# A gate projection by seven half products ahead of the convolution projection, and one weight mixture moved from VectorE to GpSimd

## The reference, cut to what matters

```python
h = rmsnorm(x, norm_mix)
cb, cc, cu, q, k, v, g, ga, gb = split(h @ w_in)
y_conv = (cb * conv3(cc * cu)) @ w_conv_out
y_ret = retention(q, k, v, g) @ w_ret_out
merged = sigmoid(ga) * y_conv + sigmoid(gb) * y_ret
x = x + merged @ w_o
h2 = rmsnorm(x, norm_mlp)
x = x + square(relu(h2 @ w_up)) @ w_down
```

## Time and profile before

| | |
|---|---|
| median of 3 executions | 2114.24 us (2113.4 to 2114.38) |
| the profiled execution | 2116.72 us, span 2114.9 us |
| granted clock of PE, mean | 0.996 of full speed |
| PE busy | 2088.9 us, 99% |
| DVE busy | 1531.7 us, 72% |
| ACT busy | 1017.3 us, 48% |
| POOL busy | 1.4 us |
| chain that ended last | PE 80%, DVE 5%, ACT 1% |

### The profile page before, as it was taken

How to read it: one execution, slowest core, us unless ns; L and a number is a source line. 1 busy time by engine, 2 the same in 40 slices (tenths; PEclk the granted TensorE clock), 3 DMA queues, 4 the chain that set the end, 5 groups by cost and what they waited for, 6 DMA issues and landing times.

```text
span 2114.9 us, 29718 instructions
## 1 busy us (share of the span) xinstructions
PE 2088.9 (99%) x11940; PEld 1869.0 (88%) x11950; DVE 1531.7 (72%) x2096; ACT 1017.3 (48%) x1456; POOL 1.4 (0%) x6
## 2 busy tenths in 40 slices
PE   9999999999999999999999999999999999999997
PEld 8888878878888899988999998888899988999996
DVE  8787785758756888756876776756779756776785
ACT  5776574645434355334553453434354334553452
POOL 0000000000000000000000000000000000000000
PEclk9999999999999999999999999999999999999998
DMA  5333222213222223422332333222223422332332
GB/s 184 110 100 101 88 80 71 90 65 100 100 80 80 86 84 120 139 90 90 120 110 87 123 110 108 92 80 80 90 81 120 140 90 90 120 110 90 120 113 77
DMA packets 59544, 212.15 MB, mean 100 GB/s; under 512 B 6736, under 2 KB 7120, under 8 KB 59280
## 3 DMA queue, kind: packets, MB, share of 16 engines
q1 hardware_dynamic: 59040, 208.83, 28.9%
q0 software_dynamic: 224, 1.31, 0.2%
q10 hardware_dynamic: 144, 0.12, 0.0%
HBM read 208.14 MB, written 2.10 MB: 99 GB/s over the span
## 4 chain that ended last, share of the span: by engine, by line
PE 80%; DVE 5%; ACT 1%; issue 1%; DMA 0%; DVEq 0%; ACTq 0%
PE bank L804 17%; PE bank L806 17%; PE bank L805 17%; PE bank L847 6%; PE bank L849 6%; PE bank L851 6%; PE bank L799 2%; PE bank L800 2%; PE bank L801 2%; DVE w_lo L1816 1%; PE bank L1050 1%; PE bank L1042 1%; ACT arena L1600 0%; PE bank L1120 0%; PE bank L1119 0%
## 5 line engine op out<-in xcount | busy, mean ns | idle before, releaser
L1816 DVE TENSOR_TENSOR w_lo<-w_raw,w_hi 128x1024 fp32r<-128x1024 f32 x459 | 551.5, 1215 | 416.6 <-ACT w_hi L1219 414.2
L1219 ACT ACTIVATE w_hi<-w_raw 128x1024 fp32r<-128x1024 f32 x459 | 474.5, 1048 | 626.9 <-PE bank L806 482.3
L804 PE MATMUL bank<-y_hi,w_hi 128*128 128x512 f32 x1048 | 399.6, 381 | 5.4 <-DVE y_lo L1870 3.4
L806 PE MATMUL bank<-y_hi,w_lo 128*128 128x512 f32 x1048 | 397.8, 380 | 0.0
L805 PE MATMUL bank<-y_lo,w_hi 128*128 128x512 f32 x1048 | 397.8, 380 | 0.0
L804 PE MATMUL bank<-h_both,w_hi 128*128 128x512 f32 x1020 | 389.5, 382 | 2.1 <-DVE arena L1865 1.1
L805 PE MATMUL bank<-h_both,w_hi 128*128 128x512 f32 x1020 | 386.6, 379 | 0.0
L806 PE MATMUL bank<-h_both,w_lo 128*128 128x512 f32 x1020 | 386.6, 379 | 0.0
L804 PEld LDWEIGHTS bank<-y_hi,w_hi 128*128 128x128 f32 x1048 | 198.4, 189 | 35.3 <-DVE w_lo L1816 4.5
L805 PEld LDWEIGHTS bank<-y_lo,w_hi 128*128 128x128 f32 x1048 | 198.5, 189 | 28.6 <-issue 0.7
L806 PEld LDWEIGHTS bank<-y_hi,w_lo 128*128 128x128 f32 x1048 | 198.5, 189 | 28.2
(11 more groups left out here) (302 smaller groups left out, 3258.4 us busy)
## 6 DMA issues: line engine op xcount, KB each, us to landing
w_raw<-in_stream SPq DMA_DIRECT2D x389, 512.0 KB, 3.5
x<-in_x_t SPq DMA_DIRECT2D x8, 256.0 KB, 7.3
out_t<-x SPq DMA_DIRECT2D x8, 256.0 KB, 2.2
arena<-in_consts POOLq DMA_DIRECT2D x1, 1024.0 KB, 5.2
w_raw<-in_stream SPq DMA_DIRECT2D x2, 256.0 KB, 4.6
arena<-in_positions POOLq DMA_DIRECT2D x1, 256.0 KB, 6.2
vec_t<-in_vecs ACTq DMA_DIRECT2D x1, 112.5 KB, 3.3
ident<-in_consts SPq DMA_DIRECT2D x1, 64.0 KB, 6.4
```

What stands on the lines that cost most here:

```text
L804: pe.matmul(out, w_hi[:, slot, w], streamed(a_h), start=first, stop=False)
L806: mm = pe.matmul(out, w_lo[:, slot, w], streamed(a_h), start=False, stop=last)
L1219: A.activation(w_hi[:, slot, w], w_raw[:, chunks.raw_slot[raw], w], ACT.Copy).then_inc(hi_ready, 1)
L1816: V.tensor_tensor(w_lo[:, slot, w], src[:, w], w_hi[:, slot, w].bitcast(F32), ALU.subtract).then_inc(lo_ready, 1)
```

## The change

Half 1 of both hybrid layers runs cc, cu, ga, cb, with ga by seven half products, as half 0 does; ga's weights come ahead of cb's in the stream. To make room, ga of half 1 keeps its two PSUM sums in `tmp2` (free once cu has used it, so ACT waits for that), and two of cb's convolution tiles of half 1 lie in unused rows of `y_lo`. The four scalings of z at the end of cu are left to ga (`owed`, in two pairs, paid between its remainders). merge, now directly behind cb, waits tile by tile. And in all seven-part steps, 24 before and 26 after, the mixture for T3 is made by GpSimd, with a semaphore of its own, `pooled`; it waits for the mixture of T1 and for its two chunks.

```diff
@@ schedule
-                Bind("half", 1, [*both(), s("cb", 4, 1), s("ga", 4, 1)]),
+                Bind("half", 1, [*both(), s("ga", 0, 1, seven=True), s("cb", 4, 1)]),
@@ taps_t, kept
-            return tmp2[:, n, :] if n < 2 else kept_rest[:, 2 * (T.fixed["turn"] % 2) + n - 2, :]
+            if n < 2:
+                return tmp2[:, n, :]
+            if T.var("half") == 1:
+                return y_lo_raw[:, (6 + n) * SEQ:(7 + n) * SEQ]
+            return kept_rest[:, 2 * (T.fixed["turn"] % 2) + n - 2, :]
...
+            if step.kind == "ga" and T.var("half") == 1:
+                return tmp2[:, n, :]
@@ gpsimd
+            for place, first, group in chunks.operand:
+                if place != T1:
+                    continue
+                upper, lower = (w_raw[:, chunks.raw_slot[first + i], :] for i in (1, 2))
+                for i in (1, 2):
+                    pool.wait_ge(raw_loaded[chunks.raw_slot[first + i]], 16 * chunks.raw_loads[first + i])
+                pool.wait_ge(combined, 3 * group + 1)
+                nc.gpsimd.tensor_tensor(upper, lower, upper, ALU.subtract).then_inc(pooled, 1)
@@ tensor
+            def cb(step):
+                T.mark["cb", T.var("half")] = T.value("a_lo")
+                of_h(step)
...
+                    elif step.kind == "merge" and first:
+                        pe.wait_ge(a_lo, T.mark["cb", k // 4] + k % 4 + 1)
...
-                def all_ready(k):
-                    if first and k == 0:
-                        pe.wait_ge(a_lo, T.value("a_lo"))
@@ scalar, raw_of and seven
-            made = {T1: 1, T3: 2, T2: 3, T4: 4}.get(place)
-            return raw + at, made and 4 * group + made
+            made = {T1: (combined, 3, 1), T2: (combined, 3, 2), T3: (pooled, 1, 1), T4: (combined, 3, 3)}.get(place)
+            return raw + at, made and (made[0], made[1] * group + made[2])
...
+                    if step.kind == "ga":
+                        act.wait_ge(vec, T.value("vec", -4))
                     keep(kept(T, step, 0), lent)
@@ vector, remainder
-                if place == T1:
-                    loaded(2)
-                    dve.wait_ge(combined, 4 * group + 1)
-                    V.tensor_tensor(raw[1], raw[2], raw[1], ALU.subtract).then_inc(combined, 1)
...
                 elif place == T1:
+                    loaded(2)
@@ vector, seven
-                    if kind != "up":
+                    if kind == "cc":
                         pay()
                     ahead(5)
                     pay(1)
                     ahead(6)
+                    pay(1)
                     ahead(7)
...
-                    got(4)
-                    dve.wait_ge(evacuated, T.value("turn", 4, 4))
-                    for n in range(4):
-                        z = z_pad[:, n, CONV2 - 1:]
-                        V.tensor_tensor(z, z, squared_rms, ALU.mult).then_inc(vec, 1)
+                    ready, read = T.value("vec", 4), T.value("turn", 4, 4)
+
+                    def scale(pair):
+                        dve.wait_ge(vec, ready)
+                        dve.wait_ge(evacuated, read)
+                        for n in (2 * pair, 2 * pair + 1):
+                            z = z_pad[:, n, CONV2 - 1:]
+                            V.tensor_tensor(z, z, squared_rms, ALU.mult).then_inc(vec, 1)
+
+                    owed.extend((lambda: scale(0), lambda: scale(1)))
```

More of the change, by code:

```diff
@@ L641, in build @@
         combined = sem("combined")
+        pooled = sem("pooled")
         seeded = sem("seeded")
@@ L978, in ready @@
                         pe.wait_ge(a_lo, T.mark["up", k // 4] + k % 4 + 1)
+                    elif step.kind == "merge" and first:
+                        pe.wait_ge(a_lo, T.mark["cb", k // 4] + k % 4 + 1)
                     elif first:
                         pe.wait_ge(a_lo, T.value("a_lo", k + 1 - n_k))
-                def all_ready(k):
-                    if first and k == 0:
-                        pe.wait_ge(a_lo, T.value("a_lo"))
-                product(step, lambda k: (y_hi[:, slot(k), :], y_lo[:, slot(k), :]),
-                        ready if step.kind in ("residual", "ret_proj") else all_ready)
+                product(step, lambda k: (y_hi[:, slot(k), :], y_lo[:, slot(k), :]), ready)
             def forget(step):
@@ L1168, in _ @@
                      "qk": of_h, "ret_scores": ret_scores, "ret_out": ret_out, "ret_turn": ret_turn,
-                     "g": of_h, "gb": of_h, "ret_proj": of_y, "cc": seven_products, "cu": seven_products, "cb": of_h,
+                     "g": of_h, "gb": of_h, "ret_proj": of_y, "cc": seven_products, "cu": seven_products, "cb": cb,
                      "ga": ga, "merge": of_y, "up": up, "mix": mix, "final": whole_norm}
@@ L1215, in round_raw @@
                 if made:
-                    act.wait_ge(combined, made)
+                    act.wait_ge(*made)
                 else:
```

## The result

The changed kernel takes **2119.36 us** (median of 17, 2116.45 to 2121.29), the kernel before, run in between, 2115.32 us (17 executions): ratio 1.0018, 95% interval 1.0011 to 1.0025. It is 4.0 us slower; 3.3 us faster was forecast. The profiled executions have the spans 2118.6 and 2114.9 us.

A forecast was written before the change was run, and what follows sets the result against it. PE, busy 2088.9 us (99% of the span), was taken as the bound. Terms: -3.9 (ga by seven) - 1.6 (scalings) + 2.2 (GpSimd's hold) = -3.3 us, giving a median of 2110.9 us, range 2108.2 to 2114.4.

The forecast's parts named there:

- ga by seven: ga of half 1, both layers: PE spends 18.76 instead of 20.72 us, -3.92 us in all.
- cb behind ga: Start of merge, directly after cb: tile-by-tile waits cost nothing; without them 3.5 us lost per layer.
- The scalings: cu's four scalings paid in ga: T3's w_lo comes 2.4 us sooner, half 0's 0.66 and 0.93 us go, -1.6 us.
- What GpSimd does to DVE: T1's remainder in seven-part groups: GpSimd's mixture either costs DVE nothing or holds it; 2.3 us hold taken, 1.1 later.
- the held case: GpSimd's mixture holds DVE's next instruction about 2.3 us, T1's remainder 1.1 later per group; the forecast itself, chance 0.47.
- Late next is T2 (slack 2.2), not late.: ga with the scalings paid there: after T3, T2's w_lo is next to be late, but its 2.2 us slack suffices.
- ACT's new wait: Before ga's first kept sum, ACT waits for cu's last product with the kept sum: costs nothing.
- Where 1.1 us hurts: Half 1, cu and ga: PE waits for w_lo 1.65 us in layer 0, 0.55 in layer 1, together 2.2 us.
- These hold: ga of half 0 and the six second up products (T3 slack 1.55, left 0.4): no PE waits from the delay.
- rival D: Weights come late into ga of half 1, both layers: PE waits 0.9 us more in each, 2112.7 us; chance 0.09.
- C: GpSimd holds DVE 3.35 us, 2.1 lost per group, second up product's T3 decides: +6.6 us, 2120.8; chance 0.08.
- A: GpSimd runs beside DVE, costing nothing or no more than 1.2 us; all slack stays: -5.5, 2108.7 us; chance 0.36.

The follow-up runs named there:

- the kernel with both mended: Changed kernel with T3's mixture back on DVE and ACT's first copy in ga not waiting for the deferred scalings: 2110.2 us, ratio 0.9974.
- the second experiment: Changed kernel with one wait shortened: ACT's first copy out of PSUM in ga no longer waits for DVE's four deferred scalings: 2114.31 us.
- GpSimd's mixture alone: Kernel before with only T3's mixture moved to GpSimd in all 24 seven-part steps: 2121.36 us, ratio 1.0027.
- the later mixture: Changed kernel with ACT's wait in ga shortened and GpSimd starting T3's mixture only after T2's mixture: 2112.36 us, ratio 0.9987.

## Why the prediction was wrong

**Right.** *ga by seven*: -3.9 in PE's time. *cb behind ga*: the tile-by-tile waits are worth the 3.5 us reckoned for them, per layer (one execution; in layer 0 the fall of the clock adds 1.7). *The scalings*: T3's waits of 0.66 and 0.93 in half 0 are gone. *What GpSimd does to DVE*: the held case, 2.38 us against 2.3 taken, 1.15 us per group against 1.1. That the size was hit so closely is in part luck: 2.3 was the middle between two DVE rows that say nothing of GpSimd. And the reason given for the held case, that both work through the same buffers, is not what decides: line 2609 is held without them. The Trainium skill (SBUF — State Buffer, Who interferes with whom) says that a DVE instruction with at most one SBUF input, outside the modes that use both port pairs, does not contend with GpSimd, and that one with two contends with a GpSimd instruction that reads SBUF. By that rule the trace agrees in both respects, 0.68 us for line 2604 and 2.64 for line 2609.

**"Late next is T2 (slack 2.2), not late."** This is the first step that failed: the scalings paid in ga stand in the sum with their gain of 1.6 us and no cost. I looked where DVE's queue goes and at the wait that the diff adds, but not at who else waits on the count that the moved scalings raise. ACT's new wait does cost nothing, as forecast: the kernel with both mended keeps it, and PE waits nowhere. An old wait, in no line of the diff, changed its meaning. It cost 0.88 and 0.87 us in ga of half 0, and 1.52 and 1.62 in ga of half 1: 4.9 us (5.05 by the experiment) where the sum had nothing; without GpSimd's hold it would have been 3.4. A wait in ga of half 0 was among the prediction's own signs of being wrong altogether.

**"Where 1.1 us hurts"** is the second. The delay was right; its places were not, for I had searched by the slack of `w_lo` alone. In half 1 it cost about 0.45 per layer (0.44 in the second experiment) instead of 2.2 in all: cu's T2, forecast to wait 0.8, did not wait, since the slow arrival of its first weights, 5.4 us in rows 6, did not recur. "These hold", of the up products, was wrong for the pairs of quarter 1, and the single up product of quarter 0 had not been looked at. Their parts' `w_lo` did hold (0.42 to 0.48 left in the pairs, 0.4 reckoned); ACT did not. In quarter 0 its rows are, in the changed kernel:

```profile
1010.70 1.06 ACT L1235 ACTIVATE w_hi<-w_raw 128x1024 fp32r<-128x1024 f32 x1 [3.90 <-DVE w_raw L1839]
1011.66 2.04 ACT L1748 ACTIVATE arena<-bank 128x512 f32<-128x512 f32 x4
1013.57 1.07 ACT L1235 ACTIVATE w_hi<-w_raw 128x1024 fp32r<-128x1024 f32 x1
1014.51 0.61 ACT L1270 ACTIVATE bank<-bank 128x512 f32<-128x512 f32 x1
```

The same rounding in the kernel before:

```profile
1008.76 1.06 ACT L1219 ACTIVATE w_hi<-w_raw 128x1024 fp32r<-128x1024 f32 x1 [2.66 <-DVE w_raw L1824]
```

T2's mixture comes late from DVE, ACT's rounding waits 3.90 us for it instead of 2.66, and behind it stand four copies of 0.5, another rounding, and only then the copy that PE needs. This copy starts 5.69 us into the stage instead of 4.82 (1012.58 before), and PE, which had lost 0.30 us in layer 0 and nothing in layer 1, loses 1.17 and 1.18. In quarter 1 the delay went through T3's remainder into the weight buffers: SP issued the next loads at 1100.11 instead of 1097.08, 1.1 us more than the stage's own shift (1071.05 against 1069.12), and ACT waited for the transfer with the kept copy behind it:

```profile
1105.98 1.06 ACT L1235 ACTIVATE w_hi<-w_raw 128x1024 fp32r<-128x1024 f32 x1 [2.75 <-DMA w_raw<-in_stream]
1106.94 0.58 ACT L1270 ACTIVATE kept_t<-bank 128x512 f32<-128x512 f32 x1
```

The later issue alone did not do it. With GpSimd's mixture alone the load was issued just as late in the stage (29.07 us into it, 29.06 here), but it landed sooner, and PE did not wait. The DMA view has the time from issue to landing of this load, in the changed kernel and then with the mixture alone:

```profile
w_raw<-in_stream SPq DMA_DIRECT2D x1, 512.0 KB, 5.8
```

```profile
w_raw<-in_stream SPq DMA_DIRECT2D x1, 512.0 KB, 3.3
```

In the kernel before it took 3.5. Why the transfer was slower is open. Late weights are what rival D named, in another place than it was looked for, and cost 1.84 us in one layer, 0.33 in the other. In all, giving the mixture back to DVE gained the changed kernel 6.05 us, where the sum had 2.2 for the hold.

**The rivals.** The measured time lies near C's 2120.8 by accident; C is not what happened: GpSimd takes 2.38, not 3.35 us, and C's deciding place, T3 of the second up product, has no wait. A is excluded by the held remainder. The range (to 2114.4) was too narrow because all of its cases shared one assumption, that ACT is never late.

With both losses mended the change is worth 5.2 us; the mixture on GpSimd has no part in it.

## What to carry to other kernels

When work is moved past a point that a semaphore counts, list every wait on that count on every engine, with what is queued behind it: a wait on "all so far" silently takes in what was moved. A delay on one engine is to be followed to each input of the bottleneck, here ACT's copies and the free buffers as well as the remainders; slack in one of them says nothing of the others. And before work is moved from DVE to GpSimd, look at what DVE runs at that moment: beside instructions with two SBUF inputs the idle gap on DVE, not GpSimd's idleness, is the room there is.

## What the runs showed of the hardware

Not expected: an instruction with one SBUF tensor as input, beside a scalar for each partition (`vec_t`), can be held as well. Behind cb of half 0, two of them at line 2460 take 3.00 us in the changed kernel; before they took 0.88 (line 2445). DVE's row of the changed kernel, then of the kernel before; GpSimd works from 818.41 to 820.86:

```profile
818.16 3.00 DVE L2460 TENSOR_SCALAR arena<-arena,vec_t 128x512 f32<-128x512 f32 x2
```

```profile
817.36 0.88 DVE L2445 TENSOR_SCALAR arena<-arena,vec_t 128x512 f32<-128x512 f32 x2
```

The same page of the Trainium skill (SBUF — State Buffer, Who interferes with whom) has this case too: a tensor_scalar can enter a fast mode that uses both port pairs, and then contends. The 0.48 us that one takes alone for 512 elements, against 0.68 of a two-input one, fits that; no run here tells the mode by itself.

The exclusion works both ways: with the later mixture GpSimd's instruction took 2.75 us instead of 2.38 where it began 0.24 us behind the start of a DVE sum of 0.75 (line 2609). And a held DVE instruction shows as a longer busy time, not as an idle gap: the group of remainders has a mean of 1262 ns after, 1215 before, and no wait names GpSimd.

```profile
L1830 DVE TENSOR_TENSOR w_lo<-w_raw,w_hi 128x1024 fp32r<-128x1024 f32 x465 | 580.5, 1262 | 411.2 <-ACT w_hi L1235 409.3 <-issue 0.8
...
L729 POOL TENSOR_TENSOR w_raw<-w_raw 128x1024 f32<-128x1024 f32 x26 | 61.8, 2377 | 1514.5 <-DVE w_raw L1835 1514.5
```

With the gap of 3.6 us ahead of merge, the granted clock was 0.50 behind it in one layer and 1.00 in the other, on the same work.
